# Softmax-merge factors of a dilated attention layer in six vector instructions and three sets, with the last chunk's probability copies and one group's weighting on ScalarE

## The reference

```
q = rotary(rms_norm(qkv[:, :, g, 0], q_norm[g]), ...); k = likewise
o, lse = dilated_window_attention(q, k, qkv[:, :, g, 2], dil, window // (2 * dil))
weights = jax.nn.softmax(jnp.stack(lses, axis=0), axis=0)
o = jnp.einsum('gbsh,gbshe->bshe', weights, jnp.stack(outs, axis=0))
y = o.reshape(B, S, ATT_WIDTH).astype(h.dtype) * jax.nn.silu(gate)
return y @ w_out
```

## Time and profile before

| | us |
|---|---|
| median of 3 runs (lowest, highest) | 1667.24 (1667.1, 1668.36) |
| the profiled execution's own time | 1666.77 |
| its span, first to last instruction | 1665.0 |
| PE busy in the span | 1651.4 |
| DVE busy | 1149.3 |
| ACT busy | 835.4 |
| POOL busy | 271.2 |

### The profile page before, as it was taken

How to read it: one execution, slowest core, us unless ns; L and a number is a source line. 1 busy time by engine, 2 the same in 40 slices (tenths; PEclk the granted TensorE clock), 3 DMA queues, 4 the chain that set the end, 5 groups by cost and what they waited for, 6 DMA issues and landing times.

```text
span 1665.0 us, 23784 instructions
## 1 busy us (share of the span) xinstructions
PE 1651.4 (99%) x8288; PEld 1402.0 (84%) x8288; DVE 1149.3 (69%) x1964; ACT 835.4 (50%) x1949; POOL 271.2 (16%) x292
## 2 busy tenths in 40 slices
PE   8999999999999999999999999999999999999999
PEld 8888888888888888888888888888888899999877
DVE  6886677787985796586868356774468336666575
ACT  6443333441441453465655246573456268895453
POOL 1000000003321100141323013240013000005440
PEclk9999999999999999999999999999999999999999
DMA  5133333484510424233332514332334656777774
GB/s 180 52 137 126 116 102 102 153 327 152 177 69 33 162 87 175 78 127 95 109 120 83 162 58 154 107 115 89 126 104 150 213 177 217 247 238 224 260 266 158
DMA packets 146134, 242.60 MB, mean 146 GB/s; under 512 B 17249, under 2 KB 55137, under 8 KB 144994
## 3 DMA queue, kind: packets, MB, share of 16 engines
q1 hardware_dynamic: 141122, 223.79, 40.2%
q10 hardware_dynamic: 4896, 17.30, 2.7%
HBM read 161.23 MB, written 79.82 MB: 145 GB/s over the span
## 4 chain that ended last, share of the span: by engine, by line
PE 97%; ACT 1%; DVE 1%; issue 0%; DMA 0%; POOL 0%; DVEq 0%
PE pair L1210 28%; PE pair L1212 28%; PE pair L1211 28%; PE pair L1562 4%; PE pair L1534 3%; PE pair L1482 2%; PE pair L1542 2%; PE pair L1231 1%; ACT pp L2695 1%; ACT qT L2688 0%; ACT turn L2746 0%; DVE pt L2225 0%; DMA ident<-in_ident_dram 0%; PE pair L1252 0%; DVE bufU L1827 0%
## 5 line engine op out<-in xcount | busy, mean ns | idle before, releaser
L1210 PE MATMUL pair<-w,turnh 128*128 128x512 f32 x640 | 249.0, 389 | 0.0
L1212 PE MATMUL pair<-w,turnl 128*128 128x512 f32 x640 | 249.0, 389 | 0.0
L1211 PE MATMUL pair<-w,turnh 128*128 128x512 f32 x640 | 249.0, 389 | 0.0
L1210 PE MATMUL pair<-w,hTh 128*128 128x512 f32 x544 | 214.0, 393 | 0.0
L1212 PE MATMUL pair<-w,hTl 128*128 128x512 f32 x544 | 212.0, 390 | 0.0
L1211 PE MATMUL pair<-w,hTh 128*128 128x512 f32 x544 | 211.7, 389 | 0.0
L2663 ACT ACTIVATE both<-pair 128x512 f32<-128x512 f32 x160 | 94.0, 592 | 175.9 <-PE pair L1212 171.8
L2152 DVE TENSOR_TENSOR both<-pair,both 128x512 f32<-128x512 f32 x120 | 81.5, 687 | 111.8 <-PE pair L1212 111.4
L2674 ACT ACTIVATE dump<-both 128x128 f32<-128x128 f32 x384 | 119.3, 311 | 63.9 <-DVE both L2152 51.4
L1210 PEld LDWEIGHTS pair<-w,turnh 128*128 128x128 f32 x640 | 120.1, 188 | 25.1 <-DVE turnl L1781 0.2
L1212 PEld LDWEIGHTS pair<-w,turnl 128*128 128x128 f32 x640 | 120.1, 188 | 25.0
(11 more groups left out here) (248 smaller groups left out, 3821.3 us busy)
## 6 DMA issues: line engine op xcount, KB each, us to landing
part_spill<-both SPq DMA_DIRECT2D x160, 256.0 KB, 3.7
both<-part_spill SPq DMA_DIRECT2D x22, 1024.0 KB, 6.0
raw_z<-in_att_w_in_dram SPq DMA_DIRECT2D x20, 1024.0 KB, 5.3
raw<-in_pool_w_in_dram SPq DMA_DIRECT2D x32, 512.0 KB, 5.2
raw<-in_att_w_in_dram SPq DMA_DIRECT2D x10, 1024.0 KB, 6.1
raw_u<-in_att_w_in_dram SPq DMA_DIRECT2D x10, 1024.0 KB, 5.9
diff_spill<-ubuf SPq DMA_DIRECT2D x16, 512.0 KB, 2.7
stage<-gate_spill SPq DMA_DIRECT2D x16, 512.0 KB, 5.7
```

Of the source, the lines that this page charges most:

```text
L1210: nc.tensor.matmul(out, lh, rh, start=first, stop=False, skip_group_check=onto)
L1211: nc.tensor.matmul(out, lh, rl, start=False, stop=False, skip_group_check=onto)
L1212: return nc.tensor.matmul(out, ll, rh, start=False, stop=last, skip_group_check=onto)
```

## The change

It does these things:

1. `factor_terms` takes two instructions in place of five, and `factors` four in place of seven (three products become one, two additions one reduction; the reciprocal and the last product stay). For that, the three groups' maxima and sums of a half lie in one tile `final`. The factors of half 1 come in three sets (blocks 0-1 at step 42, 2-4 at 45, 5-7 at 48) in place of four (42, 44, 46, 48). At step 48 `exp_factors` stands at h=0 and `factors` at h=1.
2. For rows 0 to 11 DVE weighs only the first group (512 elements). ACT weighs the second group in four instructions of 128 elements (`scale_second`, at h=1, ahead of `y_high`), and POOL waits for them before its second addition.
3. In the last chunk (heads 160 to 191) `take_pt` is ACT's, ahead of `exps`.
4. On PE `values` is that of head n-5 in place of n-4, in all chunks, and `take_u` and `store_heads` come one head later (h=0, block t-2).
5. Three halves of output weights are split one or two heads earlier (41.0, 43.0, 43.3 and so on).

```diff
-        FACTORS = {32: (0, 0, TB), 42: (1, 0, 2), 44: (1, 2, 2), 46: (1, 4, 2), 48: (1, 6, 2)}
+        FACTORS = {32: (0, 0, TB), 42: (1, 0, 2), 45: (1, 2, 3), 48: (1, 5, 3)}
-            ((40, 3), (41, 1), (41, 3), (42, 1), (43, 1), (43, 3), (44, 1), (44, 3)))})
+            ((40, 3), (41, 0), (41, 1), (41, 3), (43, 0), (43, 1), (43, 3), (44, 1)))})
...
@@ merge_rows, on POOL
                 for g in range(2):
+                    if g:
+                        pool.wait_ge(u_scaled, m + 1)
                     pool.wait_ge(pool_merged, 3 * m + g + 1)
                     nc.gpsimd.tensor_tensor(y, y, u[:, g, :], ALU.add).then_inc(pool_merged, 1)
...
@@ PE's loop
-                if 0 <= n - LAG - 1 < NHEAD:
-                    values(n - LAG - 1)
+                if 0 <= n - LAG - 2 < NHEAD:
+                    values(n - LAG - 2)
...
@@ factor_terms and factors, on DVE
-                link(nc.vector.tensor_tensor(fmin[:, at, :], s[0][:, :, 0, :], s[1][:, :, 0, :], ALU.min))
-                link(nc.vector.tensor_tensor(fmin[:, at, :], fmin[:, at, :], s[2][:, :, 0, :], ALU.min))
-                for g in range(NA):
-                    last = nc.vector.tensor_tensor(fac[:, g, at, :], fmin[:, at, :], s[g][:, :, 0, :], ALU.subtract)
-                last.then_inc(f_sub, 1)
+                link(nc.vector.tensor_reduce(fmin[:, at, :], least.rearrange("p g b h -> p b h g"), AX_X, ALU.min))
+                nc.vector.tensor_tensor(fac[:, :, at, :], fmin[:, at, :].unsqueeze(1).to_broadcast([P, NA, n, HALF]),
+                                        least, ALU.subtract).then_inc(f_sub, 1)
...
@@ merge, on DVE
-                        u4 = u.rearrange("p g (h e) -> p g h e", h=HALF)
-                        nc.vector.tensor_tensor(u4, u4, fac[:, 0:2, b, :].unsqueeze(3).to_broadcast(
-                            [P, 2, HALF, HD]), ALU.mult).then_inc(u_weighed, 1)
+                        u4 = u[:, 0, :].rearrange("p (h e) -> p h e", h=HALF)
+                        nc.vector.tensor_tensor(u4, u4, fac[:, 0, b, :].unsqueeze(2).to_broadcast([P, HALF, HD]),
+                                                ALU.mult).then_inc(u_weighed, 1)
...
@@ DVE's loop
-                if 0 <= n - LAG < NHEAD:
+                if 0 <= n - LAG < LAST_HEADS:
                     take_pt(n - LAG)
...
-                if h == 3 and t in FACTORS:
+                if h == (3 if t < NSTEP else 1) and t in FACTORS:
                     factors(*FACTORS[t])
...
@@ ACT
+            def take_pt(n):
+
+                kn = P * key_blocks(NA - 1)
+                act.wait_ge(ptr_done, n + 1)
+                act.wait_ge(pv_done, n - 3)
+                if n == LAST_HEADS:
+                    act.wait_ge(pt_ready, n)
+                nc.scalar.activation(pt[:, n % 4, 0:kn], bank(3 + n % 2)[:, 0:kn], ACT.Copy).then_inc(pt_ready, 1)
+
+            def scale_second(m):
+
+                place, loads = u_place(m)
+                act.wait_ge(uin[place], 16 * 3 * loads)
+                act.wait_ge(f_ready, factor_set(m) + 1)
+                for h in range(HALF):
+                    head = u01[place][:, 1, HD * h:HD * h + HD]
+                    last = nc.scalar.activation(head, head, ACT.Copy, scale=fac[:, 1, m % TB, h:h + 1])
+                last.then_inc(u_scaled, 1)
+
             for n in range(HALF * END):
                 t, h = n // HALF, n % HALF
+                if LAST_HEADS <= n - LAG < NHEAD:
+                    take_pt(n - LAG)
                 if 0 < n < NHEAD:
                     exps(n)
+                if h == 1 and row_at(t, 0) in ON_POOL:
+                    scale_second(row_at(t, 0))
                 if h == 1 and row_at(t, 1) is not None:
                     y_high(row_at(t, 1))
...
-                if h == 1 and t in FACTORS:
+                if h == (1 if t < NSTEP else 0) and t in FACTORS:
                     exp_factors(*FACTORS[t])
-                if h == 3 and 1 <= t <= NSTEP:
-                    take_u(t - 1)
+                if h == 0 and 2 <= t <= NSTEP + 1:
+                    take_u(t - 2)
```

More of the change, by code:

```diff
@@ L193, in encoder_program @@
                 pt = sb("pt", [P, 4, 256], F32, spare)
-                stat = sb("stat", [P, NCHUNK, TB, 2, HALF], F32, spare)
+                stat = sb("stat", [P, NCHUNK - 2, TB, 2, HALF], F32, spare)
+                fden = sb("fden", [P, NA, TB, HALF], F32, spare)
+                fmin = sb("fmin", [P, TB, HALF], F32, spare)
                 mask1 = sb("mask1", [P, 2, 256], F32, spare)
@@ L227, in encoder_program @@
             with ExitStack() as spare:
[L228 to L229 removed]
+                final = sb("final", [P, 2, NA, TB, 2, HALF], F32, spare)
                 fac = sb("fac", [P, NA, TB, HALF], F32, spare)
[L231 to L232 removed]
         HB = KD // 2
@@ L554, in last_chunk, with stat_of @@
             return CHUNKS.index((half, NA - 1))
+        def stat_of(c, b, i):
+            half, g = CHUNKS[c]
+            return final[:, half, g, b, i, :] if g == NA - 1 else stat[:, spill_number(c, 0) // TB, b, i, :]
         def spill_number(c, b):
@@ L830, in store_stat @@
                 sp.wait_ge(p_done, HALF * TB * (c + 1))
-                rows, held = st_d[g, half], stat[:, c, :, :, :]
+                rows, held = st_d[g, half], stat[:, spill_number(c, 0) // TB, :, :, :]
                 if g == 0:
@@ L841, in load_stat @@
                 sp.wait_ge(st_out[g], 16 * (half + 1))
-                sp.dma_start((st0, st1)[g][:, half, :, :, :].rearrange("p r s h -> p (r s h)"),
+                sp.dma_start(final[:, half, g, :, :, :].rearrange("p r s h -> p (r s h)"),
                              st_d[g, half].rearrange("(j r) s -> j (r s)", r=RES)).then_inc(st_in[g], 16)
@@ L2229, in factor_terms @@
                 at = slice(first, first + n)
-                s = [st0[:, half, at], st1[:, half, at], stat[:, last_chunk(half), at]]
+                least = final[:, half, :, at, 0, :]
                 for g in range(2):
@@ L2233, in factor_terms @@
                 dve.wait_ge(p_done, HALF * (TB * last_chunk(half) + first + n))
[L2234 to L2238 removed]
+                link(nc.vector.tensor_reduce(fmin[:, at, :], least.rearrange("p g b h -> p b h g"), AX_X, ALU.min))
+                nc.vector.tensor_tensor(fac[:, :, at, :], fmin[:, at, :].unsqueeze(1).to_broadcast([P, NA, n, HALF]),
+                                        least, ALU.subtract).then_inc(f_sub, 1)
             def factors(half, first, n):
                 at = slice(first, first + n)
[L2242 removed]
                 dve.wait_ge(f_exp, FACTOR_SETS.index((half, first, n)) + 1)
[L2244 to L2248 removed]
+                link(nc.vector.tensor_tensor(fden[:, :, at, :], fac[:, :, at, :], final[:, half, :, at, 1, :], ALU.mult))
+                link(nc.vector.tensor_reduce(fmin[:, at, :], fden[:, :, at, :].rearrange("p g b h -> p b h g"), AX_X,
+                                             ALU.add))
                 link(nc.vector.reciprocal(fmin[:, at, :], fmin[:, at, :]))
@@ L2274, in merge @@
                 elif part < 3:
-                    dve.wait_ge(u_scaled, 4 * k + 2 * part)
+                    dve.wait_ge(u_scaled, len(ON_POOL) + 4 * k + 2 * part)
                     dve.wait_ge(merged, 3 * k + part)
@@ L2694, in exps @@
                 act.wait_ge(masked, n + 1)
-                nc.scalar.activation(pp[:, n % 4, at], pp[:, n % 4, at], ACT.Exp, bias=stat[:, c, b, 0, h:h + 1],
-                                     scale=-1.0, accum_out=stat[:, c, b, 1, h:h + 1]).then_inc(p_done, 1)
+                nc.scalar.activation(pp[:, n % 4, at], pp[:, n % 4, at], ACT.Exp, bias=stat_of(c, b, 0)[:, h:h + 1],
+                                     scale=-1.0, accum_out=stat_of(c, b, 1)[:, h:h + 1]).then_inc(p_done, 1)
             sum_high(0)
```

17 lines of the change are left out of this document (4 added, 13 removed).

## The result

The changed kernel takes 1669.36 us (median of 22 runs, 1667.55 to 1670.98), and the kernel before 1667.28 in runs beside it (22, 1666.64 to 1668.36). The ratio is 1.0013, with a 95% interval of 1.0007 to 1.0018: **2.1 us slower**, by less than the 0.2% that I had set as the bound of "the same", but beyond the interval and in the other direction than the 1.3 us of gain that I had forecast. The profiled execution took 1668.54 us with a span of 1666.3, 1.8 and 1.3 more than before, and is the fourth fastest of the 22. The part of an execution outside its span grew too, from 1.8 us in the kernel before to 2.2, and does so in the timed runs as well.

The account below looks back on a forecast made before the run. PE bounds it, busy 1651.4 of 1665.0 us, with about 8 us of waits to win. Terms 0.6 - 0.3 + 0.2 + 0.1 - 0.8 + 1.5 = 1.3 us gained gave a median of 1666.0 us; 8-in-10 range 1662.6 to 1669.4.

Parts of the forecast that it names:

- The waits for a DVE copy: PE's nine waits for `take_pt`'s copy on DVE, from 1349 us on: gone after step 40.
- Steps 33 and 34: Later `values` and the halved DVE weighting remove the copy waits there: 0.6 us gained.
- Step 42: Without the DVE copy bank 2's chain ends earlier; PE loses 1.05 in place of 1.25: 0.2 us gained.
- Steps 43 and 44: ACT's queue replaces DVE's; PE waits about 1.5 against 1.6 in 44, 0.3 as now in 43: 0.1 us gained.
- Step 45: Four weightings on ACT before `y_high` delay bank 2; PE loses 2.7 in place of 1.9: 0.8 us lost.
- The cover of steps 36 to 41: `y_high` is 1.16 late, but a projection before bank 2's next user hides it, with 0.4 us to spare: no cost.
- Step 35: Exponential 0.9 earlier, then 1.16 of weightings; PE's queries at 1517.8 against 1517.52: 0.2 to 0.3 us lost.
- From 1616 on: Three waits behind `add_rows` and `factors` on DVE go, two projections per step covering ACT's copies: 1.5 us gained.
- The splits: The earlier output weight splits only change places within a step: cost nothing.
- The signs that I had named: No DVE-copy wait after step 40; about 1.5 in 44, 2.7 in 45; new wait in 35; none from 46.
- The first rival: Kinder row chain in steps 42 to 45, losses falling from 4.8 to about 2: 1663.5 us or less, chance 0.2.
- The second: Rival: cover of steps 36 to 41 fails as `y_high` waits behind `scale_second`: 5.4 us slower, 1671.4, chance 0.12.

Follow-up runs that it names:

- copies_values: Kernel before plus `values` one head later and the last chunk's probability copies on ACT: 1665.43 us, ratio 0.9989.
- dve_weighs_old: Changed kernel with DVE weighing both groups again and the output weights' splits at their old heads: 1663.83 us, ratio 0.9978.
- dve_weighs: Changed kernel with DVE weighing both groups in one instruction again and ACT none: 1664.20 us, ratio 0.9980.
- y_first: Changed kernel with two ACT calls swapped, `y_high` ahead of the second group's weightings: 1666.22 us, ratio 0.9995.
- second_covered: Changed kernel with ACT weighing the second group only for rows 2 to 7, 10 and 11, DVE both groups for 0, 1, 8, 9: 1664.81 us.
- filled8: Changed kernel plus 8 matmuls that serve nothing in 45.3, ahead of the queries waiting for bank 2: 1668.42 us, ratio 1.0007.
- old_splits: Changed kernel with the output weights' splits at the heads where the kernel before has them: 1668.43 us, ratio 1.0007.
- dve_copies: Changed kernel with the last chunk's probability copies on DVE again, `values` still one head later: 1670.27 us, ratio 1.0018.
- second_alone: Kernel before with only the second group of rows 0 to 11 weighed on ACT, ahead of `y_high`: 1671.61 us, ratio 1.0022.
- filled: Changed kernel plus 16 matmuls that serve nothing in 45.3, ahead of the queries waiting for bank 2: 1669.99 us, ratio 1.0018.
- values_alone: Kernel before with only `values`, `take_u` and the output stores one head later: 1666.58 us, ratio 0.9998.

## Why the prediction was off, step by step

The runs give each part a price, in us: `values` later -0.8, ACT's copies -1.2, the factors and their sets -1.6 (not run alone: it is the step from copies_values to dve_weighs_old), the splits +0.4 (without part 2) or +0.9 (with it), and the second group on ACT **+5.2**. From 1667.3 these lead to 1669.4. Everything but parts 2 and 5 is a gain of some 3.5 us. Only this gain (dve_weighs_old against before) and the price of part 2 are clear of the noise; the smaller ones are estimates.

**The step that failed is the price of the weightings on ACT.** The sum had them as -0.3 in step 35, -0.8 in step 45 and an unchanged wait in step 44, and nothing behind these waits or outside the span. dve_weighs shows 5.2 us in their place: 1.24 in step 35, 0.69 in 44, 1.29 in 45, 1.57 in 46 through the clock, and 0.44 outside the span. Taking only them out turns the loss of 2.1 into a gain of 3.1. The forecast's terms, one by one:

- **The waits for a DVE copy** are gone after step 40, as said.
- **Steps 33 and 34**: 0.79 gained, where I had 0.6.
- **Step 42**: 7.13 us became 6.91, 0.2 as forecast. **Steps 43 and 44**: 0.04 and 0.08 lost, where I had 0.1 gained. The copy that I had ready at 1599.4 started at 1599.41 and took 0.26. PE waited 1.25 for it, and 0.41 for the copies earlier in the step, where I had about 1.5.
- **Step 45**: 0.46 lost against before, where I had 0.8. Mechanism and place were right (y_first), the wait was 2.23 in place of 2.7.
- **The cover of steps 36 to 41** held: 61.61 us became 61.70. second_covered shows it too.
- **Step 35 was mis-sized, because a gain was spent twice.** I had PE's queries at 1517.8, 0.3 later than before, and they came at 1517.72. But 1517.8 is an absolute time, and I then added the 0.6 of steps 33 and 34 to these -0.3. The pair of terms is worth -0.4 in the trace (+0.79 - 1.16), where my sum had +0.3. Counted from the step's start, the four weightings are lost in full.

My reason for taking 0.9 off the exponential there was wrong as well. I said that a half weighting would no longer delay it. That the time of 1517.8 came out close is luck. The timeline of step 35:

```profile
1512.24 1.27 POOL L1208 TENSOR_TENSOR turn<-turn,both 128x512 f32<-128x512 f32 x1
...
1512.32 1.74 DVE L2266 TENSOR_TENSOR both<-both,fac 128x512 f32<-128x512 f32 x1
...
1515.16 1.26 ACT L2814 ACTIVATE both<-both,fac 128x128 f32<-128x128 f32 x4
```

The half weighting takes 1.74 us there, with POOL at work beside it, and the whole one took 1.64 before. What made the chain 0.9 earlier was only that it began 0.93 earlier (at 1512.32 in place of 1513.25), PE being ahead. That is the gain of the steps before it, which the sum so counts twice. The Trainium skill (SBUF — State Buffer, "Who interferes with whom") says that a DVE instruction with two inputs in SBUF and a GpSimd instruction that reads SBUF exclude each other; the trace agrees with 1.74 beside POOL and 0.69 in the median.

- **From 1616 on** I had 1.5 gained. Steps 47 to the end gained 0.91, since 0.36 of wait stayed and not all of the old 1.5 was lost time.
- **Missing altogether: the clock.** I priced a wait as its own length. Behind the wait of step 45 came 3.4 us at the half clock, which cost 1.6 more in the profile. filled8 shows that it hangs on PE's idleness in this place and not on the wait's cause, and y_first, dve_weighs and second_covered, which shorten the wait, have none in step 46 either.
- **Missing too: the time outside the span**, which grew by 0.44 us. The sum had no term for it. The median also lay 0.8 above the profiled execution, where I had taken 0.5.
- **The splits** I called free. They cost 0.4 to 0.9. Once ACT waits more than about 1.6 us for the load, each further us is lost in step 44.

The sum by the trace is +0.79 - 1.16 - 0.09 + 0.22 - 0.04 - 0.08 - 0.46 - 1.60 + 0.91 = -1.5 us for the steps from 33 to the end (35 is the second term, steps 36 to 41 the third, and so on). The steps ahead of them are 0.1 shorter, so the section as a whole is 1.4 longer, and with the time outside it the profiled execution is 1.8 slower. Without the clock's 1.6 that one would be about as fast as before. In the timed runs the clock is worth less: with it filled (filled8) the change is still about 1 us slower. The signs that I had named came nearly all true (no wait for a DVE copy, waits at the end of step 44, in 45 and in 35, next to none from 46 on), and the time still went the other way, since a list of waits is not the whole price. The first rival (a kinder chain) was right in direction for step 45, but not in size. The second did not come. In the first I had also miscounted: my terms for steps 42 to 45 add up to 5.6 us, not 4.8, and from 4.8 to 2 it is 2.8, not 2.5. Nothing else in the forecast rests on that. The slower outcome came by a mechanism that was none of my rivals.

**What stays open.** The half clock is in the profiled executions of the changed kernel, old_splits, dve_copies and second_alone, behind waits of 2.2, 2.2, 2.5 and 1.7 us (the last with another 1.5 and 0.7 in the same step), and not in the other ten traces. By the mean clocks of the timed runs it comes and goes in one and the same kernel. What decides is open: filled had a wait of 2.2 us in step 44, with 0.45 and 1.25 soon after it, and kept its clock, and values_alone lost it in 4 of 11 runs with a longest wait of 1.5 in its profile. Open as well is why the time outside the span grew. The price of the factors' part alone was not measured, nor whether a still later split would gain.

## What to carry to other kernels

Work put on an idle engine is free only in those steps where something long stands between it and the instruction behind it that others wait for: of twelve rows' weightings eight cost 0.6 us and four cost 4.6, and swapping two calls gives 3.1 of it back. When adding terms, ask of each whether it is a shift or an absolute time; an absolute time already holds the gains made ahead of it, and to add them again counts them twice. And price a wait of TensorE not only by its length: look at the granted clock in the windows behind it, and at the mean clock of every timed run, since one profile shows only one execution.

## What the hardware showed that I had not expected

A kernel whose PE is 99% busy can still fall to half its clock for a short time: granted 0.50 for 3.4 us behind an idle 2.2 us, 8.14 us of products taking 9.74. The Trainium skill (TensorE: Matmul & The Clock Gate, "HAM oscillation — how this bites in real kernels") describes the clock falling in a kernel that waits in every one of its tiles. Here PE had waited 0.41 and 1.25 us in the step before, and filling the 2.2 alone kept the clock up (1.00 in filled8's steps 45 and 46). That idleness brings the fall agrees; how much is needed no run here shows, as filled kept 1.00 behind 2.18.

Halving a DVE instruction did not halve it. Two views by source line, the 512-element weighting after and the 1024-element one before (least, median, longest in ns):

```profile
L2266 DVE TENSOR_TENSOR both<-both,fac x12: 685/688/1740, 1507.5 to 1618.7; 128x512 f32<-128x512 f32 x12
```

```profile
L2264 DVE TENSOR_TENSOR both<-both,fac x12: 1219/1222/1765, 1508.5 to 1617.7; 128x1024 f32<-128x1024 f32 x12
```

The median falls from 1.22 to 0.69 us and the mean only from 1.30 to 1.03. The longest stays at 1.7, and it is the longest, beside POOL, that stands on the path in step 35. ACT's copy of 128 columns out of the accumulator memory, which no trace of before showed, lasts 0.26 us, and the next instruction starts 0.16 after its start. I had taken 0.25.
